# Delta rule units: half of the backward blocks keep their half of the partitions, and backward products alternate with forward ones

## Chip, cores and metric

One core of one Trainium2 chip. The metric is the device time of one execution in microseconds, the median of several runs. The whole program is one launch: two layers of a first kind (which hold the work that changes), then two of a second kind (untouched).

## The reference, cut to what matters

Each first-kind layer mixes tokens in two branches over 512 tokens: grid attention, and a bidirectional gated delta rule with 8 heads of width 64 in chunks of 64 tokens. For each head, direction and chunk:

```
decay = exp(where(i >= j, gcum[i] - gcum[j], -inf))
a_kk  = where(i > j, (k*beta) @ k.T * decay, 0)
t_inv = inverse(eye + a_kk)                 # 64x64, unit lower triangular
u  = t_inv @ (v*beta)
w  = t_inv @ (k*beta*exp(gcum))
qk = (q @ k.T) * decay
# then over the chunks, in order:
v_new = u - w @ state
o     = (q*exp(gcum)) @ state + qk @ v_new
state = state * g_tot + (k*exp(gcum[-1]-gcum)).T @ v_new
```

The backward direction is the same rule on flipped sequences, and both outputs are added. After the mixing come an output projection and a feed-forward part. The inverse is what the change works on.

## The kernel before, in words

**Units.** In `unit(l, g, jp, r)`, l is the layer, g one of two groups of four heads, jp one of two pairs of heads in it, and r the direction (0 forward, 1 backward). A unit holds 16 blocks of 64x64: two heads, four token tiles, two chunks in a tile. Block (n, a) lies at partitions 64a to 64a+63 and columns 64n to 64n+63 of a 128x512 tile, with n = 4e + i for head e and token tile i. Its tiles X, Y, Pm, A and AT are `slot[r]`, all named s_xb in the trace; the masked tiles C are three of s_tmp.

**The inverse** is built in levels b = 1 to 5, block sizes doubling. A level has two steps on TensorE. Step P computes C'X (16 products, `eight(ps, C, X, True)`), which ScalarE copies to Pm. Step XY computes Y'Pm and Pm'Y (32 products), which VectorE subtracts from X and from Y (VectorE's TENSOR_TENSOR s_xb<-s_xb,psum). Level 5 has no X part. GpSimd makes C by masking AT. Ahead of the levels, `eight(ps, A, None, True)` turns A into AT, and GpSimd's products "X1" and "Y1" feed the first X and Y. After them, u and w are computed.

**Halves.** `one(ps, left, right, a, b, crossed)` is a 64x64x64 product from the rows of half a. Uncrossed, its result goes to the same half of the partitions, crossed, to the other. A crossed and an uncrossed one of each a are the four quarters of the TensorE array. P, X and AT are crossed for all 16 blocks, Y is uncrossed. So P and AT use two quarters, XY (crossed and uncrossed ones alternating) four. Every fp32 product is two matmul instructions and two weight loads in the trace, so that P is 32 of each and XY 64.

**Order of the work.** It is written out by hand with generators: each engine's program runs the same generators, and a `yield` ends a turn. `abreast` runs one turn of the forward units and then one of the backward ones; `delayed(..., 2)` starts the backward ones two turns later, so that both do P in one turn and XY in the next. `beside(main, fill, n, turns)` puts steps of other work behind the turns, the fill: for g = 0 the attention's steps and then projections (`project`), one step a turn; for g = 1 projections of gates (`gates`), four steps in five turns. A fill step can be empty. `plugged(main, plug, turns)` puts one of 18 halves of projections for the mixing gates (12 matmuls of 512 columns each) into the listed turns. After the units of a group, `chain` runs the recurrence over the chunks: 16 turns, with its own PSUM banks. Layer 1's order is in `mixed` (line 267 on). Here a turn is numbered from the start of a group's units: a unit has 17 turns, and its level b does P in turn 6 + 2(b-1) and XY in the turn after it; a group's second pair begins at turn 17.

**Buffers.** PSUM banks are handed out by `take` from a queue of eight in the order in which `give` returned them; `take` waits for the reader that `give` named. All instructions of TensorE are in one queue, in program order, and so are those of ScalarE, VectorE and GpSimd, each with its share of units, fill and weight splitting (`one_ahead`: ScalarE makes s_whi, VectorE s_wlo of each weight tile).

Of the kernel before, what the change touches and what calls it, by code (L numbers as in the profile page):

```python
# [176 lines left out]
class Program:  # L177
# [87 lines left out]
    def mixed(self, l, attention, scalars, begun, project, gates, plug):  # L265

        units = lambda g: abreast(self.units(l, g, 0), delayed(self.units(l, g, 1), 2))  # L270
        fill = itertools.chain(attention(), project(1, (0, 1)))
        beside(abreast(scalars, begun, delayed(project(0, (1,)), 0)), fill, 1, 1)
        beside(plugged(units(0), plug, (0, 1, 4, 5, 21, 22)), fill, 1, 1)
        beside(plugged(self.chain(l, 0), plug, (0, 1, 4, 5, 8, 9, 12, 13)), fill, 1, 1)
        for _ in fill:
            pass
        fill = gates()
        beside(plugged(units(1), plug, (4, 5, 21, 22)), fill, 5, 4)
        beside(self.chain(l, 1), fill, 5, 4)
        for _ in fill:  # L280
            pass
# [196 lines left out]
class Attn:  # L478
# [15 lines left out]
    def e(self, U):  # L494
        return self.E[:, U % self.E.shape[1], :]

# [33 lines left out]
class Tensor(Program):  # L530
# [371 lines left out]
    def unit(self, l, g, jp, r):  # L902
# [36 lines left out]
        self.eight(ps, A, None, True).then_inc(*self.up("pe_unit", key, "AT"))  # L939
        self.give((key, "AT"), ("act_unit", key, "AT"))  # L940
# [5 lines left out]
        for b in range(1, 6):  # L946
            C = self.tmp((key, "C", b))
            ps = self.take((key, "P", b))
            self.w.wait_ge(*self.at("pool_unit", key, "C", b))
            self.w.wait_ge(*self.at("vec_unit", key, "X", b - 1))  # L950
            self.eight(ps, C, X, True).then_inc(*self.up("pe_unit", key, "P", b))
            self.give((key, "P", b), ("act_unit", key, "P", b))
            yield
            self.w.wait_ge(*self.at("act_unit", key, "P", b))
            self.w.wait_ge(*self.at("vec_unit", key, "Y", b - 1))
            if b < 5:
                px, py = self.take((key, "X", b)), self.take((key, "Y", b))
                for n in range(8):
                    for a in range(2):
                        last = self.one(px, Y, Pm, a, n, True)  # L960
                        if (n, a) == (7, 1):
                            last.then_inc(*self.up("pe_unit", key, "X", b))
                        last = self.one(py, Pm, Y, a, n, False)
                last.then_inc(*self.up("pe_unit", key, "Y", b))
                self.give((key, "X", b), ("vec_unit", key, "X", b))
            else:
                py = self.take((key, "Y", b))
                self.eight(py, Pm, Y).then_inc(*self.up("pe_unit", key, "Y", b))
            self.give((key, "Y", b), ("vec_unit", key, "Y", b))
            yield  # L970
# [15 lines left out]
    def units(self, l, g, r):  # L986
        for jp in range(2):
            yield from self.unit(l, g, jp, r)

# [279 lines left out]
class Scalar(Program):  # L1269
# [380 lines left out]
    def unit(self, l, g, jp, r):  # L1650
# [15 lines left out]
        self.f(AT, self.bank((key, "AT")), ACT.Copy).then_inc(*self.up("act_unit", key, "AT"))  # L1666
        yield
        yield
        for b in range(1, 6):
            self.w.wait_ge(*self.at("pe_unit", key, "P", b))  # L1670
            self.f(Pm, self.bank((key, "P", b)), ACT.Copy).then_inc(*self.up("act_unit", key, "P", b))
            yield
            yield
# [303 lines left out]
class Vector(Program):  # L1977
# [314 lines left out]
    def unit(self, l, g, jp, r):  # L2292
# [32 lines left out]
        self.w.wait_ge(*self.at("pool_unit", key, "X1", 1))  # L2325
        self.tt(v8(X), ident, v8(Pm), ALU.subtract).then_inc(*self.up("vec_unit", key, "X", 0))
        self.w.wait_ge(*self.at("pool_unit", key, "Y1", 1))
        self.tt(v8(Y), ident, v8(Y), ALU.subtract).then_inc(*self.up("vec_unit", key, "Y", 0))
        yield
        for b in range(1, 6):  # L2330
# [4 lines left out]
            if b < 5:  # L2335
                self.w.wait_ge(*self.at("pe_unit", key, "X", b))
                self.tt(X, X, self.bank((key, "X", b)), ALU.subtract).then_inc(*self.up("vec_unit", key, "X", b))
# [356 lines left out]
class Pool(Program):  # L2694
# [5 lines left out]
    def run(self):  # L2700
# [3 lines left out]
        for l in range(2):  # L2704
# [3 lines left out]
            for g in range(2):  # L2708
                together(self.units(l, g, 0), delayed(self.units(l, g, 1), 2))
# [22 lines left out]
    def unit(self, l, g, jp, r):  # L2732
# [17 lines left out]
        if self.last is not None:  # L2750
            self.w.wait_ge(*self.at(*self.last))
        for a in range(2):
            self.tt(v8(Pm)[half(1 - a)], v8(A)[half(a)], over(MTT)[half(a)], ALU.mult).then_inc(*self.up("pool_unit", key, "X1", a))
            self.w.wait_ge(*self.at("pool_unit", key, "X1", a))
        self.last = "pool_unit", key, "X1", 1
        yield

        def block(b):
            C = self.take((key, "C", b))
            self.w.wait_ge(*self.at("act_unit", key, "AT"))  # L2760
# [5 lines left out]
        for a in range(2):  # L2766
            self.tt(v8(Y)[half(a)], v8(AT)[half(1 - a)], over(MT)[half(1 - a)], ALU.mult).then_inc(*self.up("pool_unit", key, "Y1", a))
            self.w.wait_ge(*self.at("pool_unit", key, "Y1", a))
        yield
# [224 lines left out]
```

## Time and profile before

| | us |
|---|---|
| median of 3 runs | 3276.15 (3275.21 to 3278.52) |
| the profiled execution's own time | 3268.41 |
| its span in the profile | 3266.6 |
| TensorE busy | 3134.2 (96%) |
| VectorE busy | 1881.7 (58%) |
| ScalarE busy | 1410.9 (43%) |
| GpSimd busy | 426.6 (13%) |

The units and chains stand at about 142 to 451 us of the span (first layer) and 1085 to 1440 us (second). A row of the order of time gives the start, the duration, engine, line, operation, output and inputs, how many instructions are merged in it, and in brackets the idle time ahead of it with what ended it. All matmuls of this part have line 534, so they are told apart by tiles: psum<-s_xb,s_tmp is a P step, psum<-s_xb is XY, u or w, psum<-s_cstm,s_xb is AT.

### The profile page before, as it was taken

Reading aid. Unit: us, or ns where it says so; the run is one execution under the profiler, and the core shown is the slowest. Engines: PE = TensorE matmul, PEld = TensorE weight load, DVE = VectorE, ACT = ScalarE, POOL = GpSimd, SP = SyncE. Lnnn points to the kernel's source line nnn. Section 1 sums busy time; section 2 is a strip of 40 time slices with the busy share of each in tenths; the row PEclk is TensorE's granted clock in tenths of the full one; section 3 lists DMA queues with packets and bytes.
Section 4 is the critical chain, followed back from the end, with each engine's and each line's share of the span. In section 5 each row is a group of like instructions: output and inputs, shape, how many; then the busy total and the mean of one; then the engine's idle time right before and its main releaser. Section 6 shows DMA issues by size and latency. Waiting matters only on the chain.

```text
span 3266.6 us, 59920 instructions
## 1 busy us (share of the span) xinstructions
PE 3134.2 (96%) x25776; PEld 2480.1 (76%) x25776; DVE 1881.7 (58%) x3058; ACT 1410.9 (43%) x2478; POOL 426.6 (13%) x428
## 2 busy tenths in 40 slices
PE   8899999999999999999999999999999989999999
PEld 5687778888876777878888876767788767676887
DVE  6576657756467676657745665554444655535443
ACT  5645324433246544234423355554433455444432
POOL 0051430000000332500000001121200001203010
PEclk9999999999999999999999999999999999999999
DMA  5001104333332001123333242212132232121223
GB/s 176 28 22 47 41 28 129 100 97 97 97 117 76 21 29 60 36 76 113 97 97 97 87 130 84 88 40 72 58 91 77 89 105 88 46 71 59 83 76 100
DMA packets 80216, 255.03 MB, mean 78 GB/s; under 512 B 11344, under 2 KB 13008, under 8 KB 78928
## 3 DMA queue, kind: packets, MB, share of 16 engines
q1 hardware_dynamic: 79952, 251.19, 24.7%
q8 instruction: 204, 3.34, 0.4%
q14 instruction: 60, 0.49, 0.0%
HBM read 238.08 MB, written 6.29 MB: 75 GB/s over the span
## 4 chain that ended last, share of the span: by engine, by line
PE 77%; DVE 10%; ACT 8%; issue 2%; DMA 2%; POOL 1%; SPq 1%; ACTq 0%; DVEq 0%; POOLq 0%
PE psum L534 74%; PE psum L710 3%; DVE s_wlo L1981 2%; ACT s_tmp L1277 1%; DVE s_xb L1981 1%; ACT s_whi L1277 1%; DVE s_tmp L1984 1%; DMA s_stage<-w 1%; ACT s_E L1277 1%; DVE s_ffy L1984 1%; POOL s_xb L2698 1%; SPq L2832 1%; ACT L1287 1%; DVE psum L1981 0%; ACT L1277 0%
## 5 line engine op out<-in xcount | busy, mean ns | idle before, releaser
L534 PE MATMUL psum<-s_h,s_whi 128*128 128x512 f32 (+1 forms) x4576 | 1453.6, 399 | 14.1 <-DVE s_wlo L1981 6.8
L534 PEld LDWEIGHTS psum<-s_h,s_whi 128*128 128x128 f32 (+1 forms) x4576 | 845.7, 188 | 226.7 <-issue 33.9
L534 PE MATMUL psum<-s_h,s_wlo 128*128 128x512 f32 (+1 forms) x2288 | 895.0, 391 | 0.0
L1981 DVE TENSOR_TENSOR s_wlo<-s_stage,s_whi 128x1024 fp32r<-128x1024 f32 (+2 forms) x468 | 532.5, 1140 | 358.0 <-ACT s_whi L1277 357.2
L1277 ACT ACTIVATE s_whi<-s_stage 128x1024 fp32r<-128x1024 f32 (+2 forms) x468 | 450.0, 966 | 279.9 <-DMA s_stage<-w 80.4
L534 PEld LDWEIGHTS psum<-s_h,s_wlo 128*128 128x128 f32 (+1 forms) x2288 | 430.0, 188 | 94.7
L534 PE MATMUL psum<-s_ffa,s_whi 128*128 128x512 f32 x704 | 217.5, 390 | 4.6 <-DVE s_ffa L1981 4.6
L2698 POOL TENSOR_TENSOR s_xb<-s_xb,s_cstm 64x512 f32<-64x512 f32 x64 | 101.0, 1577 | 897.6 <-DVE s_xb L1981 893.4
L2730 POOL TENSOR_SCALAR s_E<-s_E,s_inv,s_g 128x128 f32<-128x128 f32 (+3 forms) x128 | 77.0, 612 | 1058.2 <-DVE s_inv L2089 1043.5
L1984 DVE SCALAR_TENSOR_TENSOR s_ffy<-psum,s_pcol,s_ffy 128x511 f32<-128x511 f32 x176 | 131.7, 748 | 110.8 <-ACT s_ffy L1277 107.7
L1277 ACT ACTIVATE s_E<-psum,s_nm 128x256 f32<-128x256 f32 (+3 forms) x224 | 114.6, 516 | 174.8 <-DVE s_nm L2067 139.5
L534 PE MATMUL psum<-s_oR,s_whi 128*128 128x512 f32 (+1 forms) x640 | 183.4, 372 | 0.0
L2728 POOL TENSOR_SCALAR s_E<-s_E,s_inv 128x256 f32<-128x256 f32 (+3 forms) x96 | 98.3, 1039 | 495.0 <-DVE s_inv L2089 488.9
L534 PE MATMUL psum<-s_raw,s_whi 128*128 128x512 f32 (+1 forms) x480 | 153.8, 402 | 8.8 <-DVE s_raw L1984 8.4
L534 PEld LDWEIGHTS psum<-s_ffa,s_whi 128*128 128x128 f32 x704 | 131.7, 188 | 34.1 <-DVE s_ffa L1981 7.1
L1984 DVE SCALAR_TENSOR_TENSOR s_x<-psum,s_x 128x512 f32<-128x512 f32 x80 | 55.3, 691 | 161.8 <-PE psum L534 161.7
L1277 ACT ACTIVATE s_tmp<-psum 128x512 f32<-128x512 f32 (+4 forms) x126 | 70.9, 562 | 178.0 <-PE psum L534 173.9
L1981 DVE TENSOR_TENSOR s_xb<-s_xb,psum 128x512 f32<-128x512 f32 (+1 forms) x176 | 102.4, 630 | 70.5 <-PE psum L534 70.5
L534 PE MATMUL psum<-s_ffa,s_wlo 128*128 128x512 f32 x352 | 137.0, 389 | 0.0
L1277 ACT ACTIVATE s_ffy<-psum,s_pcol 128x512 f32<-128x512 f32 x88 | 60.5, 687 | 172.9 <-PE psum L534 157.2
L1277 ACT ACTIVATE s_xb<-psum 128x512 f32<-128x512 f32 x118 | 69.8, 597 | 139.0 <-PE psum L534 138.3
L534 PEld LDWEIGHTS psum<-s_oR,s_whi 128*128 128x128 f32 x640 | 114.5, 189 | 18.9
(307 smaller groups left out, 4365.5 us busy)
## 6 DMA issues: line engine op xcount, KB each, us to landing
s_stage<-w SPq DMA_DIRECT2D x192, 512.0 KB, 3.7
s_stage<-wup SPq DMA_DIRECT2D x88, 512.0 KB, 3.6
s_stage<-wo SPq DMA_DIRECT2D x32, 512.0 KB, 3.6
s_stage<-wdn SPq DMA_DIRECT2D x32, 512.0 KB, 3.6
s_stage<-wdn SPq DMA_DIRECT2D x16, 384.0 KB, 3.1
spill<-s_x SPq DMA_DIRECT2D x2, 2048.0 KB, 8.9
s_stage<-woa SPq DMA_DIRECT2D x16, 256.0 KB, 2.6
s_x<-spill SPq DMA_DIRECT2D x2, 2048.0 KB, 7.9
```

Source lines behind the costliest of these rows:

```text
L534: return self.e.matmul(out, left, right, start=first, stop=last, skip_group_check=True)
L710: last = self.e.transpose(ps[:, tile(c)], f.e(U)[:, tile(c)], m.cst[:, K_ID, :])
L1277: return self.e.activation(out, src, func, **kw)
L1287: self.e.preload_act_table_set("natural_log_exp_and_others")
L1981: return self.e.tensor_tensor(out, a, b, op)
L1984: return self.e.scalar_tensor_tensor(out=out, in0=a, scalar=s, in1=b, op0=op0, op1=op1)
L2698: return self.e.tensor_tensor(out, a, b, op)
L2728: self.e.tensor_scalar(E, E, inv, None, ALU.mult).then_inc(*self.up("pool_attn", tag, "e", U))
L2730: self.e.tensor_scalar(E, E, inv, gate(i, 2 * p + e), ALU.mult, ALU.mult).then_inc(*self.up("pool_attn", tag, "e", U))
L2832: self.e.dma_start(to[a:a + span, :], xg[b:b + span, :]).then_inc(*self.landed(f"dma_turn{n}", key, a + span))
```

## The change

The backward units (r = 1) treat their blocks n < 4 as before, and keep the results of AT, P, X of blocks n >= 4, and GpSimd's X1 and Y1, in the half in which they start (`away(r, n)`). The two kinds alternate in one step and go to two PSUM banks, so the readers (ScalarE's copies of AT and P, VectorE's subtraction of X) are cut into two instructions of 256 columns. GpSimd's X1 and Y1 of the backward units are two operations of 64x256 and one of 128x256 in place of two of 64x512. The backward units start three turns behind. The forward unit's program on TensorE (`levels`) issues the backward level steps too: in the turn of forward P(b), for b = 3 to 5, the 16 forward products alternate with the first 16 of backward XY(b-2), and the other 16 of that follow; in the turn of forward XY(b), backward P(b-1) follows. Backward XY(4) computes X with two banks and then Y alone. The chain of g = 0 gets its plugs in other turns.

```
-        units = lambda g: abreast(self.units(l, g, 0), delayed(self.units(l, g, 1), 2))
+        units = lambda g: abreast(self.units(l, g, 0), delayed(self.units(l, g, 1), 3))
-        beside(plugged(self.chain(l, 0), plug, (0, 1, 4, 5, 8, 9, 12, 13)), fill, 1, 1)
+        beside(plugged(self.chain(l, 0), plug, (3, 4, 7, 8, 11, 12, 14, 15)), fill, 1, 1)
+def away(r, n):
+    return r == 0 or n < 4
# TensorE, unit: AT
+            pn = self.take((key, "AT", 1))
+            for n in range(4):
+                for a in range(2):
+                    self.one(ps, A, None, a, n, True)
+                    last = self.one(pn, A, None, a, n + 4, False)
# TensorE, levels: the turn of forward P(b), c = b - 2 >= 1
+                px, pn, py = (self.take((two, *k, c)) for k in (("X", 0), ("X", 1), ("Y",)))
+                self.w.wait_ge(*self.at("act_unit", two, "P", c, 1))
+                self.w.wait_ge(*self.at("vec_unit", two, "Y", c - 1))
+                for k, (n, a) in enumerate(blocks):
+                    last = self.one(ps, C, X0, a, n, True)
+                    if k == 15:
+                        last.then_inc(*self.up("pe_unit", one, "P", b))
+                    if k < 8:
+                        self.one(pn, Y1, P1, near[k][1], near[k][0], False)
+                    else:
+                        self.one(py, P1, Y1, near[k - 8][1], near[k - 8][0], False)
+                for k, (n, a) in enumerate(far):
+                    last = self.one(px, Y1, P1, a, n, True)
+                    if k == 7:
+                        last.then_inc(*self.up("pe_unit", two, "X", c))
+                    last = self.one(py, P1, Y1, a, n, False)
# levels: the turn of forward XY(b), after it
+            if b > 1:
+                self.backward(two, b - 1, near, far)
# levels: backward XY(4), ahead of forward u and w
+        for k in range(8):
+            self.one(px, Y1, P1, far[k][1], far[k][0], True)
+            last = self.one(pn, Y1, P1, near[k][1], near[k][0], False)
+        last.then_inc(*self.up("pe_unit", two, "X", 4))
+        self.eight(py, P1, Y1).then_inc(*self.up("pe_unit", two, "Y", 4))
# backward: P(b)
+        for k in range(8):
+            self.one(ps, C, X1, far[k][1], far[k][0], True)
+            last = self.one(pn, C, X1, near[k][1], near[k][0], False)
# ScalarE, backward P (AT likewise)
+                for e in range(2):
+                    s = slice(256 * e, 256 * e + 256)
+                    self.f(Pm[:, s], self.bank((key, "P", e, b))[:, s], ACT.Copy).then_inc(*self.up("act_unit", key, "P", b, e))
# VectorE, backward X
+                    for e in range(2):
+                        s = slice(256 * e, 256 * e + 256)
+                        self.tt(X[:, s], X[:, s], self.bank((key, "X", e, b))[:, s], ALU.subtract).then_inc(*self.up("vec_unit", key, "X", e, b))
# GpSimd, X1 (Y1 likewise)
+        crossing = (v8, over) if r == 0 else (lambda t: v8(t)[:, 0:4], lambda k: over(k)[:, 0:4])
+        if r == 1:
+            self.tt(v8(Pm)[:, 4:8], v8(A)[:, 4:8], over(MTT)[:, 0:4], ALU.mult).then_inc(*self.up("pool_unit", key, "X1", 2))
```

## Rows read from the trace of the kernel before

**Rows 1.** The page: busy time of each engine; TensorE's clock in 40 slices.
```profile
PE 3134.2 (96%) x25776; PEld 2480.1 (76%) x25776; DVE 1881.7 (58%) x3058; ACT 1410.9 (43%) x2478; POOL 426.6 (13%) x428
...
PEclk9999999999999999999999999999999999999999
```

**Rows 2.** TensorE in order of time, units of g = 0, first pair, attention as fill.
```profile
185.13 2.08 PE L534 MATMUL psum<-s_xb,s_tmp 64*64 64x64 f32 x64
187.14 1.13 PE L534 MATMUL psum<-s_vtok,s_dno 64*128 64x512 f32 x4
...
193.59 2.08 PE L534 MATMUL psum<-s_xb,s_tmp 64*64 64x64 f32 x64
...
196.66 2.10 PE L534 MATMUL psum<-s_xb 64*64 64x64 f32 x128
198.69 1.09 PE L534 MATMUL psum<-s_ktok,s_vtok 128*64 128x128 f32 x16
...
200.73 2.08 PE L534 MATMUL psum<-s_xb,s_tmp 64*64 64x64 f32 x64
```

**Rows 3.** Instructions that touch s_xb: durations in ns, min/median/max.
```profile
L534 PEld LDWEIGHTS psum<-s_xb x5632: 129/135/135, 174.8 to 1395.9; 64*64 64x64 f32 x195
L534 PE MATMUL psum<-s_xb x5632: 212/218/268, 174.8 to 1395.9; 64*64 64x64 f32 x195
```

**Rows 4.** ScalarE and VectorE in order of time, same stretch.
```profile
194.78 0.60 ACT L1277 ACTIVATE s_xb<-psum 128x512 f32<-128x512 f32 x1 [0.49 <-PE psum L534]
196.78 1.29 DVE L2069 TENSOR_REDUCE s_nm<-psum 128x1 f32<-128x512 f32 x2 [2.83 <-PE psum L534]
198.18 0.68 ACT L1277 ACTIVATE s_x<-psum,s_nm 128x512 f32<-128x512 f32 x1
198.58 2.47 DVE L1981 TENSOR_TENSOR s_xb<-s_xb,psum 128x512 f32<-128x512 f32 x4
```

**Rows 5.** Groups by shape, VectorE and ScalarE: count, busy us, mean ns, idle before.
```profile
L1981 DVE TENSOR_TENSOR s_xb<-s_xb,psum 128x512 f32<-128x512 f32 x144 | 90.6, 680 | 70.5 <-PE psum L534 70.5
L1981 DVE TENSOR_TENSOR s_xb<-s_xb,psum 128x256 f32<-128x256 f32 x32 | 11.8, 408 | 0.0
L1277 ACT ACTIVATE s_xb<-psum 128x512 f32<-128x512 f32 x118 | 69.8, 597 | 139.0 <-PE psum L534 138.3 <-DVE s_xb L1981 0.7
L1277 ACT ACTIVATE s_wT<-psum 128x256 f32<-128x256 f32 x16 | 6.1, 383 | 0.0
```

**Rows 6.** TensorE in order of time, g = 0, second pair, projections as fill.
```profile
238.20 2.25 PE L534 MATMUL psum<-s_xb,s_tmp 64*64 64x64 f32 x61 [0.89 <-DVE s_xb L1981]
...
246.22 2.34 PE L534 MATMUL psum<-s_xb,s_tmp 64*64 64x64 f32 x64 [0.87 <-DVE s_xb L1981]
...
254.13 2.10 PE L534 MATMUL psum<-s_xb 64*64 64x64 f32 x128 [0.78 <-ACT s_xb L1277]
256.18 2.52 PE L534 MATMUL psum<-s_xb,s_tmp 64*64 64x64 f32 x61
```

**Rows 7.** VectorE in order of time, same stretch, ahead of 246.22.
```profile
243.96 1.52 DVE L1984 SCALAR_TENSOR_TENSOR s_tmp<-psum,s_pcol,s_tmp 128x511 f32<-128x511 f32 x2
245.40 2.47 DVE L1981 TENSOR_TENSOR s_xb<-s_xb,psum 128x512 f32<-128x512 f32 x4
```

**Rows 8.** TensorE in order of time, g = 1, first pair, gates as fill.
```profile
372.77 2.25 PE L534 MATMUL psum<-s_xb,s_tmp 64*64 64x64 f32 x61 [1.38 <-DVE s_xb L1981]
...
385.15 2.08 PE L534 MATMUL psum<-s_xb,s_tmp 64*64 64x64 f32 x64
```

**Rows 9.** Who TensorE waited for, 140 to 430 us: total, times, longest.
```profile
PE psum L534 <- issue: 5.5, 5, 1.8
PE psum L534 <- DVE s_xb L1981: 4.7, 6, 1.4
```

**Rows 10.** TensorE's waits in the first layer's first chain.
```profile
303.00 0.48 PE L534 MATMUL psum<-s_S,s_qd 64*64 64x64 f32 x16 [0.77 <-ACT s_dno L1277]
329.02 0.63 PE L621 MATMUL psum<-s_cst,s_tmp 128*128 128x128 f32 x4 [1.35 <-DVE s_tmp L1984]
```

More of the change, by code:

```diff
@@ L945, in unit @@
         yield
[L946 to L952, printed above, removed]
-            yield
[L954 to L969, printed above, removed]
+        if r == 0:
+            yield from self.levels(l, g, jp)
+        else:
+            for _ in range(8):
+                yield
+            self.last_level(l, g, jp, False)
+            yield
+            self.last_level(l, g, jp, True)
             yield
@@ new lines, in backward @@
+    def backward(self, two, b, near, far):
+        X1 = self.m.slot[1][0]
+        ps, pn, C = self.take((two, "P", 0, b)), self.take((two, "P", 1, b)), self.tmp((two, "C", b))
+        self.w.wait_ge(*self.at("pool_unit", two, "C", b))
+        self.w.wait_ge(*self.at("vec_unit", two, "X", 1, b - 1))
+        for k in range(8):
+            self.one(ps, C, X1, far[k][1], far[k][0], True)
+            last = self.one(pn, C, X1, near[k][1], near[k][0], False)
+        last.then_inc(*self.up("pe_unit", two, "P", b))
+        for e in range(2):
+            self.give((two, "P", e, b), ("act_unit", two, "P", b, e))
@@ new lines, in last_level @@
+    def last_level(self, l, g, jp, update):
+        two = (l, g, jp, 1)
+        Y1, P1 = self.m.slot[1][1:3]
+        blocks = [(n, a) for n in range(8) for a in range(2)]
+        if not update:
+            self.backward(two, 5, [k for k in blocks if not away(1, k[0])], [k for k in blocks if away(1, k[0])])
+            return
+        py = self.take((two, "Y", 5))
+        self.w.wait_ge(*self.at("act_unit", two, "P", 5, 1))
+        self.w.wait_ge(*self.at("vec_unit", two, "Y", 4))
+        self.eight(py, P1, Y1).then_inc(*self.up("pe_unit", two, "Y", 5))
+        self.give((two, "Y", 5), ("vec_unit", two, "Y", 5))
@@ L1670, in unit @@
             self.w.wait_ge(*self.at("pe_unit", key, "P", b))
-            self.f(Pm, self.bank((key, "P", b)), ACT.Copy).then_inc(*self.up("act_unit", key, "P", b))
+            if r == 0:
+                self.f(Pm, self.bank((key, "P", b)), ACT.Copy).then_inc(*self.up("act_unit", key, "P", b, 1))
+            else:
+                for e in range(2):
+                    s = slice(256 * e, 256 * e + 256)
+                    self.f(Pm[:, s], self.bank((key, "P", e, b))[:, s], ACT.Copy).then_inc(*self.up("act_unit", key, "P", b, e))
             yield
@@ L2324, in unit @@
         self.w.wait_ge(*self.at("vec_unit", key, "q", 1))
[L2325 to L2327 removed]
+        self.w.wait_ge(*self.at("pool_unit", key, "X1", 1 + r))
+        self.tt(v8(X), ident, v8(Pm), ALU.subtract).then_inc(*self.up("vec_unit", key, "X", 1, 0))
+        self.w.wait_ge(*self.at("pool_unit", key, "Y1", 1 + r))
         self.tt(v8(Y), ident, v8(Y), ALU.subtract).then_inc(*self.up("vec_unit", key, "Y", 0))
@@ L2336, in unit @@
                 self.w.wait_ge(*self.at("pe_unit", key, "X", b))
-                self.tt(X, X, self.bank((key, "X", b)), ALU.subtract).then_inc(*self.up("vec_unit", key, "X", b))
+                if r == 0:
+                    self.tt(X, X, self.bank((key, "X", b)), ALU.subtract).then_inc(*self.up("vec_unit", key, "X", 1, b))
+                else:
+                    for e in range(2):
+                        s = slice(256 * e, 256 * e + 256)
+                        self.tt(X[:, s], X[:, s], self.bank((key, "X", e, b))[:, s], ALU.subtract).then_inc(*self.up("vec_unit", key, "X", e, b))
             else:
@@ L2708, in run @@
             for g in range(2):
-                together(self.units(l, g, 0), delayed(self.units(l, g, 1), 2))
+                together(self.units(l, g, 0), delayed(self.units(l, g, 1), 3))
                 self.chain(l, g)
@@ L2766, in unit @@
         for a in range(2):
-            self.tt(v8(Y)[half(a)], v8(AT)[half(1 - a)], over(MT)[half(1 - a)], ALU.mult).then_inc(*self.up("pool_unit", key, "Y1", a))
+            some, masks = crossing
+            self.tt(some(Y)[half(a)], some(AT)[half(1 - a)], masks(MT)[half(1 - a)], ALU.mult).then_inc(*self.up("pool_unit", key, "Y1", a))
             self.w.wait_ge(*self.at("pool_unit", key, "Y1", a))
+        if r == 1:
+            self.tt(v8(Y)[:, 4:8], v8(AT)[:, 4:8], over(MT)[:, 0:4], ALU.mult).then_inc(*self.up("pool_unit", key, "Y1", 2))
         yield
```

63 lines of the change are left out of this document (58 added, 5 removed).

## The prediction, made before the changed kernel was run

> **What bounds the kernel now.** I read the page first: TensorE is busy 96% of the span at the full granted clock, 2.4 GHz, in all slices, VectorE 58%, ScalarE 43% [rows 1]. A busy TensorE need not be a well used one, so the next view was the order of time in the stretches that change. With the attention as fill, instructions stand back to back and no wait shows; a P turn (two units, 64 instructions) lasts from 185.13 to 187.14, 2.01 us, and an XY turn (two units, 128 instructions) from 196.66 to 198.69, 2.03 us [rows 2]. The reader is to see that: half as many products take the same time. That is 31.4 ns an instruction where two quarters of the array alternate, and 15.9 ns where four do. The view of waits says how near the other engines are: over the first layer's units and chain TensorE waited 4.7 us for VectorE's s_xb and 5.5 us for nothing that the profile shows [rows 9]. So this part is bound by TensorE's issue, with a thin margin, and it is TensorE time that the change takes away.
>
> **What is removed.** A step of 16 products costs 1.00 us on two quarters (half of 2.01) and 32/128 of 2.03, 0.51 us, on four. For each of the 8 pairs of a forward and a backward unit (2 layers, 2 groups, 2 jp) the change moves to four quarters: backward AT (1 step), backward P(1) to P(5) (5), and forward P(3) to P(5), each of which alternates with half of a backward XY (3). Nine steps by 0.49 is 4.4 us. Against it: backward XY(4) issues its 16 Y products alone, on two quarters, 1.00 in place of 0.51, so 0.49 back. Net 3.9 us a pair, 31.5 us in all. Forward P(1), P(2), all Y(5), u and w keep their pattern. The number of matmuls is the same. A merged turn comes to 96 instructions, 1.52 us, against 2.01 and 2.03 before. The streams' patterns (crossed, uncrossed of one half, then of the other, into two banks) are those of XY, so I take XY's rate.
>
> A rule of the Trainium skill speaks against this. The row first: a weight load lasts 135 ns and a matmul 218 ns [rows 3], and the XY stream starts one every 15.9 ns although each crossed product is followed by an uncrossed one from the same rows of the array. The Trainium skill, TensorE: Matmul & The Clock Gate, section The mechanism, says that a weight load overlaps with running matmuls only when its row group differs. By it, pairing products of the same rows would win nothing and the 31.5 us would be 0; the trace disagrees for the very same order of quarters.
>
> **What is added on the readers.** Backward AT and P are copied in two instructions: a 256-column ScalarE copy takes 0.38 against 0.60 for 512, so 0.77 in place of 0.60, 0.17 more, 48 times, 8 us of ScalarE. Backward X(1) to X(4) in two subtractions: 2 x 0.41 against 0.68, 0.14 more, 32 times, 4.5 us of VectorE [rows 5]. Both lie beside TensorE's work where the turn has fill, and count only in the waits below. GpSimd's X1 and Y1 are not shown at the new shapes; between nothing and the whole of one step they move the backward unit's start only, which has a spare turn now. I take 0. More banks are taken in a period of two turns (8 by the units in place of 6), so that a bank comes back after about seven takes; going through the order, each is read by then, the nearest being forward Y's with some 0.2 us to spare where the attention holds one bank. Between 0 and 0.5 us a pair; it goes into the first case below.
>
> **Waits that the shorter turns uncover.** Here I chose, because the trace has no such turn. Write A for a turn with forward P and backward XY, B for one with forward XY and backward P. What must be ready when A starts: forward X (its products end 1.02 into B, VectorE takes 0.68 and some 0.2 pass about it [rows 5]: B+1.9) and backward P in Pm (products end at B+1.52, two copies 0.77, about 0.2: B+2.5). What B needs: forward P (the last of it leaves 1.0 into A, the copy starts 1.19 after the start in the trace: P at 193.59 [rows 2], copy 194.78 to 195.38 [rows 4]: A+1.9). Turns now last 1.52.
>
> - Attention as fill (first pair of g = 0, one a layer): some 1.06 us of scores after A (the step at 187.14), 2.04 of the rest after B (198.69 to 200.73) [rows 2]. B begins at A+2.58 against 1.9 needed. A begins at B+3.56; VectorE's maxima and subtractions there ran 196.78 to 201.05, and ScalarE's second exponential ends at B+2.2 (198.18 + 0.68 - 196.66) [rows 4], with the two copies behind it B+3.1. Covered; 0.5 a pair for banks and queues.
> - Projections as fill (second pair of g = 0): six of the gaps between level turns hold no work. B to A without fill waits 2.5 - 1.52 = 1.0, twice; A to B 1.9 - 1.52 = 0.4, once; forward P(2) now stands alone ahead of its XY(2), 0.9; where TensorE waits already 0.87 because VectorE has convolution taps ahead of the subtractions (243.96, then 245.40 [rows 7]), it arrives about 0.5 to 1 us earlier and waits longer, 0.8 over two places. One wait shrinks: P(2) waited 0.89 for X(1) [rows 6] and has backward AT in front of it now, -0.5. Sum 3.6 a pair.
> - Gates as fill (g = 1, two pairs a layer): one gap in five is empty. At 385.15 such turns stood with no wait [rows 8]; two of these a pair cost 1.0 and 0.4. The 1.38 at 372.77 is VectorE's, behind a split of weights, and grows by about 0.5. Sum 1.9 a pair.
>
> Together 2 x 0.5 + 2 x 3.6 + 4 x 1.9 = 15.8 us. Bounds: 0, if the fill's own slack moves over (TensorE's other waits shrink when it comes earlier only at 0.5 of 4 places, so this is far), and 0.9 us, the size of the waits that stand in rows 6, in each of the 60 level turns without attention: 54 us. I take 15.8, near the rows that stand in this very order.
>
> **Turn three and the plugs.** The third turn of delay puts one more turn at the end of each group in which the backward unit stands alone, with fill in it: 0.3 each, 1.2 us. The chain's plugs go to turns 3, 4, 7, 8, 11, 12, 14, 15; the projections' steps run out one turn earlier in it. The turns where it waited were those without either (0.77 at 303.00 after turn 3, others shorter); now turns 2, 6, 10 and 13 are bare, the first three of which only wait for VectorE's v. The 1.35 at 329.02 is a projection's own tail [rows 10] and stays. Between -2 and +2 a layer; I take -0.6 a layer.
>
> **Sum.** -31.5 + 15.8 + 1.2 - 1.2 = -15.7 us. Against the profiled execution's own time of 3268.41, 3252.7; that execution lies 7.7 below the median of the runs shown, so the median becomes 3276.15 - 15.7, 3260.
>
> **Rivals.** 0.2% of this kernel, 6.6 us, is about what can be told from no change.
>
> *The whole gain* arrives (chance 0.08): VectorE and ScalarE find their time inside the fill and the added waits stay under 5 us. 3276 - 31.5 + 3 is 3248. For it: no wait at all in the attention's stretch [rows 2]. Against: the waits in rows 6.
>
> *A new wait takes its place* (0.14): TensorE's queue is in order, and merging ties two chains together: one late copy stops both. At 25 to 38 us of waits over the 80 level turns (0.3 to 0.5 a turn) nothing can be measured: 3270 to 3282, middle 3276.
>
> *Slower by lockstep* (0.09). The same coupling, as the mechanism that wins: a merged turn starts with the later of forward X and backward Pm, which is copied in two pieces behind the fill's work on ScalarE. Its place is the 60 level turns with projections and gates, its price 0.7 us each (rows 6: 0.78 to 0.89 where it happens now), 42 us; it decides from 31.5/60, 0.53 us a turn. 3276 - 31.5 + 42 is 3287. For it: VectorE and ScalarE already end four of the waits in rows 6 and 8. Against: fill of 1.5 us or more stands in most gaps.
>
> *It doesn't do what it says* (0.05): the alternation of products of two units with three banks runs at the old 31.4 ns. Then nothing is saved but the cost of Y(4) (8 x 0.49 in the case that only the old pattern is quick) and about 6 us of waits: 3286. The Trainium skill's rule quoted above is one way to it; the 15.9 ns speak against.
>
> The forecast has 0.64, with its own range of 3250 to 3269.
>
> **Chances and range.** Faster by over 0.2% (below 3269.6): 0.64 + 0.08 and a little of the second rival, 0.73. Within 0.2%: 0.13. Slower (above 3282.7): 0.14. The range goes from the whole gain to the middle of the second rival: 3246 to 3277.
>
> **What would show it.** In the changed profile: TensorE's instruction count unchanged at 25776 and its busy time about 30 us less; merged turns of 96 instructions in about 1.5 us in the attention's stretch, with no wait; backward AT in 0.5 us. The view of waits: s_xb by VectorE and ScalarE together up by some 16 us over both layers, most of it with projections and gates, where ScalarE's second half-copy of backward P is what ends it. ScalarE busy up by 8, VectorE by 4. Wrong it would be if merged turns took 2 us, if waits appeared in the attention's stretch (banks), or if the waits' growth passed 30 us.

## Result and profile after

| | before | after |
|---|---|---|
| median, us | 3275.68 (3272.84 to 3278.52) | 3312.67 (3311.45 to 3314.78) |
| profiled execution's own time | 3268.41 | 3313.51 |
| its span | 3266.6 | 3311.7 |
| mean granted clock | 0.997 | 0.988 |

The change makes the kernel slower: ratio 1.0114, 95% interval 1.0101 to 1.0127, 37 us. 3260 was forecast, with a range to 3277, and the dearest rival stood at 3287. The two profiled executions lie 45.1 us apart. The one of the kernel before was a quick one: its mean granted clock of 0.997 stands above the 0.991 to 0.996 of that kernel's executions beside the experiments, and plugs and late_before (below), as fast as before within 0.1%, show TensorE busy for 3142.8 and 3141.9 us at 0.994.

**The page after** (busy time by engine; TensorE's clock in 40 slices). Against [rows 1], TensorE's busy time is 5.6 us up, where 30 down was forecast, its share is down from 96 to 95%, and a slice of the clock reads 8. Against the 3142 of plugs and late_before it is some 2 us down.
```profile
PE 3139.8 (95%) x25776; PEld 2474.1 (75%) x25776; DVE 1869.7 (56%) x3090; ACT 1413.3 (43%) x2526; POOL 410.5 (12%) x444
...
PEclk9998999999999999999999999999999999999999
```

**By stretch, first layer.** Each line of these windows covers one part of the order of work: g = 0 first pair, g = 0 second pair, its chain, g = 1 first pair, second pair. The columns are length, busy time and count of TensorE, its weight loads, VectorE, ScalarE and GpSimd, then the granted clock, the DMA share and GB/s. Before:
```profile
142.50:210.00 67.50, 66.77 (x1453) 53.05 (x1454) 45.44 (x71) 30.73 (x67) 29.70 (x20) 1.00 0.07 19
210.00:288.90 78.90, 72.99 (x1551) 60.67 (x1546) 57.05 (x75) 37.16 (x55) 28.35 (x18) 1.00 0.12 36
288.90:341.00 52.10, 48.97 (x615) 39.20 (x615) 29.00 (x56) 21.06 (x32) 4.59 (x12) 1.00 0.19 55
341.00:394.80 53.80, 51.03 (x1247) 42.93 (x1244) 37.41 (x50) 16.70 (x27) 31.41 (x20) 1.00 0.13 40
394.80:459.90 65.10, 59.76 (x1449) 49.95 (x1449) 38.68 (x52) 19.04 (x32) 26.44 (x18) 1.00 0.11 35
```
After:
```profile
144.20:215.00 70.80, 63.91 (x1425) 49.94 (x1425) 42.28 (x74) 30.80 (x72) 27.28 (x22) 1.00 0.06 18
215.00:309.10 94.10, 78.01 (x1574) 63.40 (x1574) 54.47 (x84) 37.83 (x62) 24.44 (x20) 0.91 0.10 30
309.10:361.50 52.40, 49.49 (x611) 38.66 (x611) 26.93 (x54) 21.05 (x32) 5.60 (x12) 1.00 0.18 52
361.50:415.00 53.50, 48.14 (x1210) 39.25 (x1210) 37.09 (x51) 16.29 (x31) 30.03 (x22) 1.00 0.14 42
415.00:479.30 64.30, 57.25 (x1479) 47.25 (x1478) 39.62 (x58) 19.84 (x40) 25.82 (x20) 1.00 0.12 36
```
The second line is where the time went: 15.2 us longer, and its clock is 0.91, which means that for about 17 us of it TensorE ran at the lower of its levels, 1.2 GHz, in place of 2.4. The first line is 3.3 us longer although TensorE is busy 2.9 less. In the last two the saving is there (2.9 and 2.5 us of busy time) and the idle time beside it grew by nearly as much. The second layer repeats this: its second stretch is 16.0 us longer. The last pair of the kernel before runs to 459.9, so that [rows 9], which end at 430, leave out its end. The five stretches sum to 17.7 and 22.3 us more; the rest of the 45.1 lies in code that didn't change.

**Who TensorE waited for, whole span** (total us, times, longest). Before:
```profile
PE psum L534 <- DVE s_xb L1981: 10.7, 14, 1.4
...
PE psum L534 <- DVE s_tmp L1984: 5.3, 3, 1.9
...
PE psum L534 <- ACT s_xb L1277: 3.0, 4, 0.8
```
After (lines 1981 and 1984 are now 2085 and 2088, 534 is 539, 1277 is 1372):
```profile
PE psum L539 <- DVE s_xb L2085: 26.2, 27, 2.2
PE psum L539 <- DVE s_tmp L2088: 24.0, 9, 4.1
...
PE psum L539 <- ACT s_xb L1372: 12.2, 22, 1.3
```
The two s_xb together rise from 13.7 to 38.4, where 16 more were forecast, and a wait that the forecast doesn't have, for VectorE's s_tmp, rises from 5.3 to 24.0, up to 4.1 us at a time.

**What that wait is.** TensorE in order of time, g = 0, second pair, after:
```profile
252.34 1.02 PE L539 MATMUL psum<-s_h,s_whi 128*128 128x512 f32 x2 [3.54 <-DVE s_tmp L2088]
...
270.54 1.13 PE L539 MATMUL psum<-s_xb,s_tmp 64*64 64x64 f32 x32 [1.84 <-DVE s_tmp L2088]
...
290.90 1.14 PE L539 MATMUL psum<-s_xb,s_tmp 64*64 64x64 f32 x32 [3.25 <-DVE s_tmp L2088]
```
VectorE ahead of the first:
```profile
249.00 1.74 DVE L2085 TENSOR_TENSOR s_xb<-s_cstm,s_xb 128x512 f32<-128x512 f32 x1 [1.42 <-POOL s_xb L2807]
250.67 1.52 DVE L2088 SCALAR_TENSOR_TENSOR s_tmp<-psum,s_pcol,s_tmp 128x511 f32<-128x511 f32 x2
```
Neither a projection (252.34) nor a P step (290.90) reads the projections' s_tmp. What they need is a bank, and the bank that comes round is one that a projection filled and that VectorE's convolution taps still read; the profile names no bank, so experiments 1, 4 and 5 test this reading. The taps stand in VectorE's queue behind an operation that waited 1.42 us for GpSimd.

**The clock after such an idle stretch.** TensorE behind the wait at 290.90 (a projection's 12 matmuls of 512 columns), after:
```profile
291.97 1.22 PE L539 MATMUL psum<-s_h,s_whi 128*128 128x512 f32 x2
...
296.83 0.44 PE L539 MATMUL psum<-s_h,s_wlo 128*128 128x512 f32 x1
```
and the same 12 before, at the full clock:
```profile
248.50 0.73 PE L534 MATMUL psum<-s_h,s_whi 128*128 128x512 f32 x2
...
251.14 0.39 PE L534 MATMUL psum<-s_h,s_wlo 128*128 128x512 f32 x1
```
From first to last row 4.86 us in place of 2.64. The granted clock of the stretches shows the low level at and behind the waits; after:
```profile
270.00:280.00 10.00, 9.46 (x147) 7.63 (x148) 5.14 (x9) 6.03 (x8) 1.29 (x1) 0.68 0.01 2
280.00:290.00 10.00, 6.78 (x200) 5.54 (x199) 5.46 (x10) 3.44 (x7) 0.00 (x0) 1.00 0.19 57
290.00:300.00 10.00, 9.10 (x84) 7.19 (x85) 4.02 (x6) 5.43 (x7) 0.00 (x0) 0.66 0.00 0
```
TensorE looks almost fully busy where it is slow. That is why its busy time rose in this stretch (215.00 to 309.10) by 5.0 us, although the same work takes 71.02 us, 2.0 less than before, when the clock stays full (late, below).

### The profile page after: what moved, and what is told of

Same layout as the page of the kernel before. It is cut to its first block, busy times and chain, and to the rows that moved or that the text cites. A ratio compares the mean times of both kernels' runs of the same rounds, so it can differ in the third digit from the quotient of the medians.

```text
span 3311.7 us, 60014 instructions
## 1 busy us (share of the span) xinstructions
PE 3139.8 (95%) x25776; PEld 2474.1 (75%) x25776; DVE 1869.7 (56%) x3090; ACT 1413.3 (43%) x2526; POOL 410.5 (12%) x444
## 3 DMA queue, kind: packets, MB, share of 16 engines
q1 hardware_dynamic: 79952, 251.19, 24.7%
## 4 chain that ended last, share of the span: by engine, by line
PE 77%; DVE 9%; ACT 7%; issue 2%; POOL 2%; DMA 1%; SPq 1%; ACTq 0%; DVEq 0%; POOLq 0%
PE psum L539 74%; PE psum L715 2%; DVE s_xb L2085 2%; POOL s_xb L2807 2%; ACT s_tmp L1372 1%; DVE s_tmp L2088 1%; DVE s_wlo L2085 1%; ACT s_whi L1372 1%; DMA s_stage<-w 1%; ACT s_E L1372 1%; SPq L2949 1%; POOL s_tmp L2807 1%; ACT s_xb L1372 1%; ACT L1382 1%; ACT L1372 0%
## 5 line engine op out<-in xcount | busy, mean ns | idle before, releaser
L539 PE MATMUL psum<-s_h,s_whi 128*128 128x512 f32 (+1 forms) x4576 | 1464.1, 401 | 23.0 <-DVE s_tmp L2088 7.6
L539 PEld LDWEIGHTS psum<-s_h,s_whi 128*128 128x128 f32 (+1 forms) x4576 | 852.3, 190 | 236.0 <-issue 40.5
L539 PE MATMUL psum<-s_h,s_wlo 128*128 128x512 f32 (+1 forms) x2288 | 899.9, 393 | 0.5 <-issue 0.5
L539 PEld LDWEIGHTS psum<-s_h,s_wlo 128*128 128x128 f32 (+1 forms) x2288 | 433.1, 189 | 97.0 <-issue 0.9
L539 PE MATMUL psum<-s_ffa,s_whi 128*128 128x512 f32 x704 | 217.4, 390 | 4.6 <-DVE s_ffa L2085 4.6
L2807 POOL TENSOR_TENSOR s_xb<-s_xb,s_cstm 64x512 f32<-64x512 f32 (+2 forms) x80 | 89.3, 1117 | 925.8 <-DVE s_xb L2085 920.8
L539 PE MATMUL psum<-s_oR,s_whi 128*128 128x512 f32 (+1 forms) x640 | 183.4, 372 | 0.0
L539 PE MATMUL psum<-s_raw,s_whi 128*128 128x512 f32 (+1 forms) x480 | 154.4, 403 | 7.9 <-DVE s_raw L2088 7.9
L539 PEld LDWEIGHTS psum<-s_ffa,s_whi 128*128 128x128 f32 x704 | 131.7, 188 | 34.3 <-DVE s_ffa L2085 7.1
L539 PEld LDWEIGHTS psum<-s_xb 64*64 64x64 f32 x5632 | 121.6, 134 | 44.3 <-issue 19.0
L539 PE MATMUL psum<-s_xb 64*64 64x64 f32 x5632 | 135.2, 221 | 19.4 <-ACT s_xb L1372 8.6
L1372 ACT ACTIVATE s_xb<-psum 128x256 f32<-128x256 f32 (+1 forms) x166 | 72.3, 472 | 180.7 <-PE psum L539 180.7
L539 PE MATMUL psum<-s_ffa,s_wlo 128*128 128x512 f32 x352 | 137.0, 389 | 0.0
```

What stands on the lines that cost most here:

```text
L539: return self.e.matmul(out, left, right, start=first, stop=last, skip_group_check=True)
L1372: return self.e.activation(out, src, func, **kw)
L2807: return self.e.tensor_tensor(out, a, b, op)
```

## Experiments

Each ratio is to the kernel before, run on the same chip, with its 95% interval. The kernels ran on several chips, so they are compared with each other by their ratios, and a difference of two ratios is uncertain by 4 to 9 us. "Late" means one edit, the same everywhere: the bank of a projection is put back into the queue two turns later, so that a unit doesn't meet it while the taps read.

**1. The banks alone.** Before, with the second bank of backward P and X taken and given back, but not used.
```
+            if r == 1:
+                self.take((key, "P", b, "idle"))
             self.eight(ps, C, X, True)...
+                self.give((key, "P", b, "idle"), ("act_unit", key, "P", b))
# X likewise
```


> The kernel before, with nothing changed but PSUM bookkeeping: each backward P step and each backward X step also takes a second bank from the queue, does not write it, and gives it back with the same reader as the first. The computation is complete. Theory 1 (bank turnover: TensorE waits because a bank comes round again before its reader has emptied it, since the units take 8 banks in two turns and not 6): slower by 8 to 25 us, with new waits of TensorE for VectorE's convolution taps (s_tmp<-psum,s_pcol) in the second pair of g = 0. Theory 2 (lockstep: the merged turns wait for data of two chains): within 3 us of the kernel before. Theory 3 (the clock alone): no change unless waits come first.

Measured 1.0034 [1.0022, 1.0046], +11 us, with nothing else changed: inside the 8 to 25 us of Theory 1. TensorE in its second stretch shows the wait that the kernel before doesn't have there:
```profile
246.28 1.98 PE L534 MATMUL psum<-s_xb 64*64 64x64 f32 x64 [4.17 <-DVE s_tmp L1993]
```
and its waits by VectorE:
```profile
PE psum L534 <- DVE s_tmp L1993: 17.2, 7, 4.2
...
PE psum L534 <- DVE s_xb L1990: 6.9, 8, 1.3
```

**2. The delay with the plugs, and the plugs alone.**
```
-delayed(self.units(l, g, 1), 2)
+delayed(self.units(l, g, 1), 3)          # d3_plugs only
-(0, 1, 4, 5, 8, 9, 12, 13)
+(3, 4, 7, 8, 11, 12, 14, 15)             # both
```


> The kernel before with the backward units three turns behind and the chain's plugs in the changed kernel's turns; steps, halves and banks as before. Theory 1: the kq banks are held one turn longer and the backward g bank is read a turn later, so it costs 5 to 15 us, in both pairs of g = 0. Theory 2: the delay only costs one turn at the end of each group, 0 to 4 us.

> The kernel before with only the chain's plugs moved to the changed kernel's turns. All theories: between -3 and +3 us; it is run to take the plugs out of the account of the delay.

Measured: d3_plugs 1.0051 [1.0035, 1.0067], +17 us; plugs 1.0007 [0.9997, 1.0016]. The plugs cost nothing, and the third turn, priced at 1.2 us, costs about 15. Waits of d3_plugs:
```profile
PE psum L534 <- DVE s_xb L1981: 19.9, 19, 1.9
...
PE psum L534 <- ACT s_xb L1277: 7.6, 10, 1.3
```
So the delay alone gives more than half of the growth of the s_xb waits (27.5 against 13.7 before and 38.4 after).

**3. Everything but the alternation**, at two turns of delay (apart2) and at three with the new plugs (apart3). Backward X goes to two banks on four quarters, then Y alone.
```
+                for k in range(8):
+                    self.one(px, Y, Pm, far[k][1], far[k][0], True)
+                    last = self.one(pn, Y, Pm, near[k][1], near[k][0], False)
+                self.eight(py, Pm, Y)
```


> Backward blocks kept in their halves with two banks and split reads, as in the changed kernel, but two turns behind, the plugs where they were, and no step alternating with one of the other direction (backward X alternates far and near, its Y follows alone on two quarters). By the rates of the kernel before it takes 8 x (6 - 4) x 0.49 = 8 us off TensorE. Theory 1: the second banks cost more than that, 0 to 17 us slower. Theory 2: no merged turn, so the saving shows, -8 to -2 us.

> The changed kernel with its delay of three turns, halves, banks and plugs, but without the alternation: each direction's steps are issued on their own, forward P on two quarters, backward Y alone on two. It has 4 x (3 x 0.49 + 3 x 0.49) = some 24 us more of TensorE time than the changed kernel by the rates of the kernel before. Theory 1: the bank takes are the same, so the loss against before is that of the second banks (11 us) and of the delay (16 us) less 8 us of saving: 3290 to 3300, and the alternation itself gives little or takes up to 20. Theory 2: the merged turns are the cause, so this one is 20 us or more below the changed kernel, at 3285 or less.

Measured: apart2 1.0042 [1.0027, 1.0057], +14; apart3 1.0107 [1.0085, 1.013], +35. Nearly all of the loss is there with no product of the two directions alternated. But apart3 lies above both of its expected ranges (3290 to 3300, and 3285 or less): the prices of 1 and 2 with the 8 us of saving add up to 18, and 35 came.

**4. The banks' return moved**, in after (late) and in before (late_before).
```
-        self.give(key, ("vec_proj", key, "y", 4))
         yield
         yield
+        self.give(key, ("vec_proj", key, "y", 4))
```


> The changed kernel, with the PSUM bank of each projection of queries, keys and values given back to the queue two turns later, so that the units reach it after VectorE's four convolution taps have read it. Computation complete. Theory 1 (bank turnover): the waits for s_tmp fall from 24 us to about 5, the clock's falls in g = 0 go with them, and the time is 15 to 30 us below the changed kernel's, 3283 to 3298. Theory 2 (lockstep of data): the waits move to s_xb, within 5 us of the changed kernel.

> The kernel before with the same later return of the projections' banks. Theory 1: its waits for the taps are already few (5.3 us), so between -5 and +3 us against the kernel before. Theory 2: the same.

Measured: late 1.0048 [1.0032, 1.0064], 22 us below after; late_before 0.9995 [0.9985, 1.0004]. Late's waits:
```profile
PE psum L539 <- DVE s_xb L2085: 33.6, 32, 2.2
...
PE psum L539 <- ACT s_xb L1372: 12.0, 20, 1.3
```
The row of L539 for VectorE's s_tmp is gone, s_xb takes up 7 of its 24 us. The second stretch is 82.1 us in place of 94.1, at the full clock:
```profile
214.10:296.20 82.10, 71.02 (x1577) 58.36 (x1577) 55.39 (x84) 37.74 (x62) 25.19 (x20) 1.00 0.12 35
```
With the same work in it, TensorE's busy time there falls from 78.01 to 71.02 us. So of the 12.0 us that the return takes off this stretch, 7.0 are work done at the low clock, and 5.0 are idle time.

**5. Second banks with the late return, and apart3 with it.** The edits of 1 and 3, with that of 4.

> The kernel before with idle second banks for backward P and X (as in banks) and the projections' banks given back two turns later. Theory 1 (bank turnover, at the projections' banks): the 11 us of banks go, -4 to +4 us against the kernel before, and TensorE's wait for s_tmp falls from 17 to about 5 us. If other banks matter as much: +7 us or more.

> The changed kernel without the alternation and with the projections' banks given back two turns later; to be compared with late, which alternates. By the measured turns the alternation takes 16 to 20 us off TensorE. Theory 2 (lockstep: the merged turn waits for data of both directions, so the saving turns into waits): late is at most 6 us below this one. Theory 1 alone: late is 12 us or more below it.

Measured: banks_late 0.9998 [0.9989, 1.0007]; apart3_late 1.0059 [1.0042, 1.0076]. The 11 us of the second banks are the projections' banks, within the 3 us that the interval leaves. The late return takes 16 us off apart3 and 22 off after, at three turns, and 9 off apart2 (experiment 8), at two; with it the parts do add up: apart3_late's 19 us are about the delay's 15 and the 4 of apart2_late. And against apart3_late the alternation of late is worth 4 us by the ratios (2 by the medians, of two chips), within 8 us either way, though TensorE's busy time falls by 14.5, from 3144.1 to 3129.6. The s_xb waits are 10.9 us longer in late, 45.6 against 34.7.

**6. One turn of delay**: before with it (d1), and the change rebuilt for it with the old plugs, forward P(b) beside backward XY(b-1) (merged1, merged1_late).
```
-delayed(self.units(l, g, 1), 2)
+delayed(self.units(l, g, 1), 1)
# merged1: in levels
-                c = b - 2
+                c = b - 1
```


> The kernel before with the backward units one turn behind in place of two; nothing else. Theory 1 (bank turnover): the kq banks are held a turn less than before and the backward g bank is read a turn earlier, so none of the waits of the three-turn delay at the start of g = 0: between -6 and +4 us. If an odd delay as such costs (P of one direction beside XY of the other, so that the steps and VectorE's and ScalarE's work alternate), it is slower by 10 us or more, like three turns.

> The change built on a delay of one turn: forward P(b) alternates with backward XY(b-1) for b = 2 to 5, backward P(b) follows forward XY(b), backward Y(4) is inside a merged turn; the plugs are where they were in the kernel before. By the rates it takes 8 x 10 x 0.4 = some 32 us off TensorE. Theory 1: the delay's part of the loss goes (some 15 us), the second banks' part (10 us and the waits for the taps) stays: -10 to +8 us against the kernel before. Theory 2 (lockstep): the merged turns' waits for s_xb stay and eat the saving, +10 us or more.

> As the kernel before this one in the list (merged, one turn behind), and the projections' banks given back two turns later. Theory 1: without the waits for taps and the clock falls that follow them, the saving shows: -22 to -8 us against the kernel before. Theory 2: no better than 0.

Measured: d1 1.0083 [1.0067, 1.01], +27; merged1 1.0092 [1.0077, 1.0107]; merged1_late 1.0063 [1.0048, 1.0079]. All three missed Theory 1, by which one turn would cost nothing: I took the loss at three turns for banks that are held longer and read later, and one turn costs still more. What the expectation of d1 set against it, that an odd delay as such costs 10 us or more, fits both. Two is the best of the three delays. TensorE in d1's units shows s_xb waits such as
```profile
244.83 1.05 PE L534 MATMUL psum<-s_xb,s_tmp 64*64 64x64 f32 x29 [2.76 <-DVE s_xb L1981]
```
and VectorE ahead of it
```profile
243.39 0.69 DVE L1981 TENSOR_TENSOR s_xb<-s_cstm,s_xb 128x512 f32<-128x512 f32 x1 [3.86 <-POOL s_xb L2698]
244.00 1.28 DVE L1981 TENSOR_TENSOR s_xb<-s_xb,psum 128x512 f32<-128x512 f32 x2
```
The subtraction that TensorE needs stands in VectorE's queue behind an operation that waited 3.86 us for GpSimd's X1 or Y1. Over the whole span d1's VectorE has
```profile
DVE s_xb L1981 <- POOL s_xb L2698: 40.2, 18, 3.9
```
where the same row is 14.4 before and 27.2 in d3_plugs: the order of the times (0, +15, +27). So the rows point at GpSimd's first products of the two directions, which two turns of delay would keep apart best. No run moved these products alone, so this isn't shown. Merging at one turn is neither gain nor loss against d1 (3 us more, within 7), and the late return takes 9 off it, but neither wins back the 27.

**7. Backward g and gq a turn later** in late (g_later_late).
```
# TensorE, unit, ahead of the products g and gq
+        if r == 1:
+            yield
# and one of the two yields behind them only for r == 0
```


> As late, and the backward unit's first products (g, gq) are issued one turn later, after forward AT, so that AT takes banks that have been read. Theory 1 for the delay: the waits of 1.6 and 1.3 us in front of AT at the start of g = 0 go, 5 to 12 us below late. Otherwise within 3 us of late.

Measured 1.0024 [1.0014, 1.0034], 8 us below late, within 6. This answers two waits in the attention's stretch, where the forecast saw none. After:
```profile
164.06 1.15 PE L539 MATMUL psum<-s_cstm,s_xb 64*64 64x64 f32 x32 [1.61 <-DVE s_xb L2085]
166.49 0.70 PE L539 MATMUL psum<-s_h,s_whi 128*128 128x512 f32 x2 [1.28 <-ACT s_xb L1372]
```
The AT step at 164.06 isn't held by A, which VectorE had written by 159.65. It starts when this read of the backward g ends, and g's bank is read until then:
```profile
158.95 0.70 DVE L2085 TENSOR_TENSOR s_xb<-s_xb,psum 128x256 f32<-128x256 f32 x2
...
163.32 0.68 DVE L2085 TENSOR_TENSOR s_xb<-psum,s_scgc 128x512 f32<-128x512 f32 x1
```
In g_later_late neither wait is there. VectorE's waits for GpSimd's s_xb fell with them (21.8 in late, 14.7 here), so the 8 us needn't be the bank's alone.

**8. The alternation at the old delay.** Backward Y(b) is put off into the next P turn, where its products alternate with forward P's; halves, two banks, late return, old plugs. two_turns_late has it, apart2_late is the same without alternation, and two_turns_g_later adds the edit of 7.
```
# levels, the turn of forward P(b), c = b - 2 >= 1
+                py = self.take((two, "Y", c))
+                for n, a in blocks:
+                    self.one(py, P1, Y1, a, n, False)
+                    last = self.one(ps, C, X0, a, n, True)
+            if b > 1:
+                self.backward(two, b - 1, near, far)
# the turn of forward XY(b), after it: backward X(b-1) into two banks
```


> Another way to the same saving, backward units two turns behind as in the kernel before: backward blocks kept in their halves with two banks, but backward Y(b) is put off into the next P turn, where its 16 uncrossed products alternate with the 16 crossed ones of forward P; backward P and X run on four quarters on their own; plugs as before; projections' banks given back two turns later. By the measured turns 8 x 3.3 = 26 us less TensorE time. If the loss is bank turnover and the odd delay (theory 1): 10 to 22 us below the kernel before. If every shorter turn only turns into waits for data (theory 2): -4 us or worse.

> Halves, two banks and split reads at the old delay of two turns, with the projections' banks returned two turns later and nothing alternated. Same delay and same return as two_turns_late (-6 us against before), so the difference is the alternation. If TensorE's saving from alternation arrives (3 forward P and 3 backward Y a pair, 6 x 0.49 x 8 pairs, 23 us), this is 3274 - 6 + 23 = 3291. If most of it turns into waits for s_xb as at three turns, where it was worth 2 to 4 us, this is 3270 to 3272. I expect 3272: apart2 was +14 and the return took 11 to 16 off kernels with second banks.

> two_turns_late, and the backward units issue their products g and gq one turn later. At three turns the same edit took 8 us off, because backward AT retook the bank of g before VectorE had read it. If that wait stands at two turns too: 3268 - 4 to 8 = 3260 to 3264. If the two turns leave the bank read in time, the later g only delays the backward unit's first levels: 3268 to 3274. I expect 3266.

Measured: two_turns_late 0.9981 [0.9971, 0.999], -6 us, where Theory 1 had -10 to -22; apart2_late 1.0015 [1.0006, 1.0024], +4; **two_turns_g_later 0.9969 [0.9957, 0.9982], 3264.0 against 3272.76 us: it beats both kernels.** At two turns the alternation is worth 11 us by the ratios (within 4), so my 3272 for apart2_late was too low. The page's busy times and the row of waits for s_xb, of apart2_late:
```profile
PE 3143.7 (96%) x25776; PEld 2484.1 (76%) x25776; DVE 1889.1 (58%) x3090; ACT 1411.6 (43%) x2526; POOL 418.2 (13%) x444
```
```profile
PE psum L539 <- DVE s_xb L2120: 9.6, 13, 1.3
```
and of two_turns_late:
```profile
PE 3123.5 (96%) x25776; PEld 2463.9 (75%) x25776; DVE 1887.4 (58%) x3090; ACT 1411.5 (43%) x2526; POOL 420.5 (13%) x444
```
```profile
PE psum L539 <- DVE s_xb L2076: 19.9, 25, 2.2
```
20.2 us of TensorE's time go, and 10.3 come back as waits for VectorE's s_xb. Halves without alternation take none of TensorE's time (3143.7 at a mean clock of 0.992; late_before, without them, 3141.9 at 0.994), where 8 us less were expected of apart2; so against late_before this version takes 18 us off it. XY turns of apart2_late are longer, because Y alone runs on two quarters:
```profile
186.84 1.61 PE L539 MATMUL psum<-s_xb,s_tmp 64*64 64x64 f32 x64
...
189.44 2.59 PE L539 MATMUL psum<-s_xb 64*64 64x64 f32 x128
191.97 1.09 PE L539 MATMUL psum<-s_ktok,s_vtok 128*64 128x128 f32 x16
```
A P turn is 1.54 us there, 0.47 less than [rows 2], an XY turn 2.53, 0.50 more: six savings a pair against four losses.

## Why the prediction was wrong, point by point

Two terms of the sum failed, both of them near nothing in it: the second banks and the third turn of delay.

- **"Between 0 and 0.5 us a pair" for banks: wrong, the larger failure.** The prediction looked for the nearest bank where the attention holds one, and readers are prompt there. In the projections' stretch one of the eight banks is held by VectorE's taps. Two more takes in each period of two turns bring it round too early. Shown by banks (+11 us), banks_late (nothing) and late (22 us back from after). At 4.17 and 3.54 us one such wait is seven to eight times the term's upper end; the clock that falls behind it adds to the price. In the first layer's second stretch 7.0 of the 12.0 us that the late return wins are the clock. No rival of the prediction had banks as its mechanism; only its signs of being wrong named them, and for the attention's stretch.
- **"1.2 us" for the third turn of delay: wrong by a factor of 12.** I priced the turn at the end of the group, not what three turns do to who meets whom. d3_plugs less plugs is 15 us. Part of it, in the changed kernel, is at the bank of backward g, which forward AT meets before its reader: moving g won 8. The prediction also put GpSimd's X1 and Y1 at 0, because the backward unit has a turn to spare; VectorE's waits for them are 14.4 us before, 27.2 in d3_plugs, 21.7 in after and 40.2 in d1. That these are the rest of the 15, and the 27 of one turn, fits the rows and stays open.
- **Plugs at -1.2 us**: measured +1.5 by the medians, -1 to +5 by the interval. Right within what can be told.
- **The saving, 31.5 us of TensorE's time: right in kind, too large.** A merged turn without a wait inside lasts from 189.75 to 191.31, 1.56 us, 1.52 forecast; after:
```profile
189.75 0.21 PE L539 MATMUL psum<-s_xb,s_tmp 64*64 64x64 f32 x1 [0.91 <-DVE s_xb L2085]
...
191.31 0.70 PE L539 MATMUL psum<-s_vtok,s_dno 64*128 64x512 f32 x2
```
A lone step on four quarters takes 0.57 us right behind an XY step (185.17 to 185.74) and 0.62 to 0.63 elsewhere, not 0.51, and forward P alone 1.08 (182.05 to 183.13) in place of 1.00:
```profile
179.37 0.69 PE L539 MATMUL psum<-s_cstm,s_xb 64*64 64x64 f32 x32 [0.60 <-ACT s_x L1372]
180.00 1.09 PE L539 MATMUL psum<-s_ktok,s_vtok 128*64 128x128 f32 x16
...
182.05 1.15 PE L539 MATMUL psum<-s_xb,s_tmp 64*64 64x64 f32 x32
...
185.17 0.65 PE L539 MATMUL psum<-s_xb,s_tmp 64*64 64x64 f32 x32
```
Six lone steps a pair at 0.06 to 0.12 more and two at 0.08 are 0.5 to 0.9 of the 3.9; the stretches at the full clock show 2.5 to 2.9 less.
- **The rule of the Trainium skill** (TensorE: Matmul & The Clock Gate, The mechanism), by which pairing products of the same rows would win nothing: the merged turn's 1.56 us for 96 instructions, 16 ns each, stands against it again. The same section names a second way, a load into the background weight buffer; no run here shows whether that is what happens. The rival by which merged turns run at the old rate is refuted.
- **15.8 us of uncovered waits: too small.** s_xb waits grew by 24.7 in after, by 32 in late, where the bank waits no longer cover them. The lockstep rival (0.7 us in 60 turns) had a mechanism that the waits fit once the banks are mended: late against apart3_late, 14.5 us less of TensorE's time and 10.9 more of s_xb waits. But the delay alone makes 13.8 of the 32 (d3_plugs). It isn't what made after slow, since apart3, with no product of the two directions alternated, is as slow.
- **"Covered" in the attention's stretch: wrong.** That stretch became 3.3 us longer. A shorter turn brings TensorE also to the attention's own steps early; at this transpose of the exponential, after, it waits where it didn't:
```profile
188.19 0.66 PE L715 MATMUL psum<-s_cst,s_x 128*128 128x128 f32 x4 [0.76 <-ACT s_x L1372]
```
- **ScalarE's 8 us and VectorE's 4.5 of split reads: too large, and not the cause.** ScalarE's busy time rose by 2.4 us and VectorE's fell by 12.0: two copies of 256 columns in a row take 0.66 us (31.6 us for 48 pairs) in place of 0.77, and VectorE's products of s_ktok into s_xb went from 1325 to 679 ns, which no run explains. banks_late and late_before, without the splits, don't tell their price, and apart2_late bounds it: halves, splits and all cost 4 us over before.

## What to carry to other kernels

In a queue of banks, count the takes between a slow reader's bank and its return in the stretch where that reader is slowest, not where it is prompt; a wait that names data which the waiting instruction doesn't read is a bank, and returning that bank later in the order was the remedy here. Changing a delay between two programs that share queues moves every meeting in it, so measure the delay alone before building on it. Time taken from the bounding engine arrives only as far as the engines it feeds on keep up: here some 11 of 20 us at two turns, and 4 of 14.5 at three, within 8, so that even whether three turns keep less isn't clear of the noise.

## What was unexpected of the hardware

- An idle stretch of 1.8 to 3.5 us in TensorE's queue cost more than itself here: behind the waits at 270.54 and 290.90 the granted clock of ten microseconds is 0.68 and 0.66, and 12 matmuls took 4.86 us in place of 2.64. It isn't a matter of one long wait alone: in late, the projection at 163.71, behind waits of 1.60 and 1.28, shows the long durations too. And not each such wait brings it: behind d1's 2.76 at 244.83 the next projection, at 249.64, has its first two matmuls in 0.74 us, the full clock's duration.
- Four quarters give 16 ns an instruction only in long bursts; 32 instructions alone took 0.57 to 0.63 us, 18 to 20 ns each.
- The profiles differ by some us in code that is the same in all, with the clock lower than the 0.997 of before's (0.994 in plugs and late_before, 0.992 in late and two_turns_g_later, 0.993 in two_turns_late). What sets this is open; effects of 5 us are near it.
